# Matrix-memory layer of a three-part decoder: gates as rows, convolution beside the gate branch, heads normalised from PSUM; attention transposes through four banks

## Reference

```python
def mlstm_mixer(u, w_in, conv_w, conv_b, wq, wk, wv, w_gates, b_gates, norm_w, skip, w_out):
    xm, z = jnp.split(u @ w_in, 2, axis=-1)                 # 2048 wide each
    xc = jax.nn.silu(causal_depthwise_conv(xm, conv_w, conv_b))   # 4 taps
    q, k, v = block_diag_proj(xc, wq), block_diag_proj(xc, wk), block_diag_proj(xm, wv)
    gates = q @ wg_q + k @ wg_k + v @ wg_v + b_gates        # 6144 -> 8: 4 heads, i and f
    i_pre, f_pre = jnp.split(gates, 2, axis=-1)
    log_f = jax.nn.log_sigmoid(f_pre)
    h = mlstm_chunkwise(...)       # running sum and running maximum of the gates over the tokens,
                                   # decay matrix from them, scores q k^T times decay, times v,
                                   # divided by max(|row sum|, exp(-m))
    # each head of 512: (h - mean) * rsqrt(var + eps), per token
    h = (h * norm_w + skip * xc) * jax.nn.silu(z)
    return h @ w_out
```

## Time and profile before

| | |
|---|---|
| median of 3 runs | 3438.85 us (3420.95 to 3454.4) |
| the profiled execution | 3429.66 us, of which the span of instructions 3427.9 us |
| PE busy | 3193.9 us, 93% of the span |
| DVE, ACT busy | 1022.8 us (30%), 473.2 us (14%) |
| DMA | 732.26 MB, mean 214 GB/s |
| mean granted clock of TensorE | 0.959 of full speed |

### The profile page before, as it was taken

The page is one execution under the profiler, slowest core; times in us unless marked ns, Lnnn a source line. Parts: engine busy times, 40 slices in busy tenths (PEclk is TensorE's granted clock), DMA queues, the critical chain, the costliest instruction groups (busy, mean ns, idle before and its releaser), DMA issues.

```text
span 3427.9 us, 56270 instructions
## 1 busy us (share of the span) xinstructions
PE 3193.9 (93%) x24082; PEld 2691.2 (79%) x24083; DVE 1022.8 (30%) x2204; ACT 473.2 (14%) x1077; POOL 15.1 (0%) x26
## 2 busy tenths in 40 slices
PE   5999999999999999999998768997679999999998
PEld 4888888888888888888887757886666887668875
DVE  5213222320221322242035253368431111111113
ACT  1001112100100111210001200005320111101110
POOL 0000000000000000000000000000000000000000
PEclk8999999999999999999999669999889999999999
DMA  8646534364464563436446205760329788898884
GB/s 331 245 160 250 197 130 178 123 246 184 156 260 162 212 230 136 178 123 245 184 160 258 101 0 188 300 262 1 125 95 353 298 325 318 314 352 326 329 320 189
DMA packets 55190, 732.26 MB, mean 214 GB/s; under 512 B 6576, under 2 KB 6760, under 8 KB 10516
## 3 DMA queue, kind: packets, MB, share of 16 engines
q1 hardware_dynamic: 51092, 716.69, 54.7%
q0 software_dynamic: 3968, 13.74, 1.2%
HBM read 729.32 MB, written 4.23 MB: 214 GB/s over the span
## 4 chain that ended last, share of the span: by engine, by line
PE 81%; DMA 8%; DVE 7%; issue 2%; ACT 1%; SPq 0%; DVEq 0%; POOL 0%; ACTq 0%; POOLq 0%
PE psum L639 48%; PE psum L1041 11%; PE psum L1084 9%; PE psum L626 2%; PE psum L696 2%; DMA ring<-in_up_dram 2%; DMA ring<-in_up_e_dram 2%; DVE ring L1424 2%; PE psum L817 1%; PE psum L1065 1%; PE psum L1100 1%; DMA ring<-in_down_e_dram 1%; DMA ring<-in_w_qk_dram 1%; DVE work L1943 1%; DMA ring<-in_ada_dram 1%
## 5 line engine op out<-in xcount | busy, mean ns | idle before, releaser
L639 PE MATMUL psum<-h_t,ring 128*128 128x256 f32 x5888 | 1291.6, 382 | 31.2 <-DVE h_t L1570 8.8
L639 PEld LDWEIGHTS psum<-h_t,ring 128*128 128x128 f32 x5888 | 1124.3, 191 | 197.6 <-issue 29.0
L639 PE MATMUL psum<-work,ring 128*128 128x256 f32 x2752 | 603.4, 382 | 21.8 <-ACT work L1255 10.2
L639 PEld LDWEIGHTS psum<-work,ring 128*128 128x128 f32 x2752 | 526.7, 192 | 96.8 <-ACT work L1255 10.6
L1041 PE MATMUL psum<-h_t,ring 128*64 128x96 f32 x11264 | 471.7, 247 | 5.9 <-DMA ring<-in_up_e_dram 5.6
L1041 PEld LDWEIGHTS psum<-h_t,ring 128*64 128x64 f32 x11264 | 467.8, 137 | 9.1 <-issue 7.8
L1084 PE MATMUL psum<-ring,work 128*96 128x512 f32 x704 | 304.1, 593 | 0.6 <-DMA ring<-in_down_e_dram 0.5
L1424 DVE SCALAR_TENSOR_TENSOR ring<-ring,cond 128x1024 f32<-128x1024 f32 x240 | 279.2, 1220 | 36.5 <-DMA ring<-in_ada_dram 35.4
L1084 PEld LDWEIGHTS psum<-ring,work 128*96 128x96 f32 x704 | 114.1, 163 | 184.9 <-issue 183.1
L1487 DVE TENSOR_TENSOR work<-work,psum 128x256 f32<-128x256 f32 (+1 forms) x118 | 49.7, 421 | 624.2 <-PE psum L639 609.3
L2235 DVE TENSOR_TENSOR work<-work,psum 128x256 f32 x176 | 74.2, 421 | 403.8 <-PE psum L1041 403.8
(11 more groups left out here) (326 smaller groups left out, 1652.2 us busy)
## 6 DMA issues: line engine op xcount, KB each, us to landing
ring<-in_up_e_dram SPq DMA_DIRECT2D x64, 2048.0 KB, 7.7
ring<-in_ada_dram SPq DMA_DIRECT2D x60, 2048.0 KB, 7.8
ring<-in_up_dram SPq DMA_DIRECT2D x55, 2048.0 KB, 7.9
ring<-in_down_e_dram SPq DMA_DIRECT2D x32, 1792.0 KB, 8.5
ring<-in_down_dram SPq DMA_DIRECT2D x20, 2816.0 KB, 9.6
ring<-in_up_e_dram SPq DMA_DIRECT2D x32, 1536.0 KB, 8.4
ring<-in_down_e_dram SPq DMA_DIRECT2D x16, 2048.0 KB, 8.9
ring<-in_w_qk_dram SPq DMA_DIRECT2D x12, 2048.0 KB, 8.6
```

Of the source, the lines that this page charges most:

```text
L639: mm = pe.matmul(half(b), w, moving(k, j * lin.groups + m), start=(k == 0), stop=(k == depth - 1))
```

## The change

Matrix-memory mixer: z has no ada chunks; `m_out` has four instead (with one chunk of its own ahead). DVE makes the convolution in four parts of four tiles during z, and ACT puts silu of part j-1 behind z's chunk j, of the last two parts behind chunk 3. The gate products come before `vtok`: the gate weights (128x4, input or forget gates) are stationary and the 128x256 activation tiles move; four results, for two tiles and two gates, go to partitions 0, 32, 64, 96 of bank 4. Weights and `tri` are fetched at the start of z, into `rms` and `skip`; the rows lie in `h`. ACT copies three of the four partial rows, DVE adds them. The skip scaling of `xc` stands ahead of the gates on DVE. PE's order is then `vtok`, scores of heads 0 and 1, `rows_t`, scores of heads 2 and 3. In the numerator PE goes head by head; DVE takes statistics straight from PSUM, and ACT writes (h - mean) * scale from PSUM (`Identity` with bias and scale). Head transposes go to banks 4 to 7, the product with silu(z) is made tile by tile, and `m_out` waits for one tile at a time. Attention: the transposes rotate through banks 4 to 7, and each v product waits for its own head.

```diff
-    mix = uses(b4=4, b5=4, b6=1, b7=1)
+    mix = uses(b4=2, b5=2, b6=3, b7=3)
...
-        "xm": Linear(4, 4, 32 * P, "m_xm", 4, 1, biased=4), "z": Linear(4, 4, 32 * P, "m_z", 4),
+        "xm": Linear(4, 4, 32 * P, "m_xm", 4, 1, biased=4), "z": Linear(4, 4, 32 * P, "m_z"),
...
-        "m_out": Linear(4, 2, 32 * P, "m_out"), "ln0": ln_after,
+        "m_out": Linear(4, 2, 32 * P, "m_out", 4, 1), "ln0": ln_after,
...
                 for n in range(HG):
-                    b = 4 + n % 2
+                    b = LIN + n % LIN
                     pe.wait_ge(signal["probs"], lp.of("probs", n + 1))
-                    pe.wait_ge(bank_free[b], reads(p, b, n // 2))
+                    pe.wait_ge(bank_free[b], reads(p, b, n // LIN))
...
-                pe.wait_ge(bank_free[4], reads(p, 4, 4))
-                pe.wait_ge(bank_free[5], reads(p, 5, 4))
-                pe.wait_ge(bank_free[6], reads(p, 6))
-                pe.wait_ge(bank_free[7], reads(p, 7))
+                pe.wait_ge(bank_free[6], reads(p, 6, 2))
                 for n in range(HG):
                     e = (g * HG + n) * HD
+                    pe.wait_ge(bank_free[LIN + n % LIN], reads(p, LIN + n % LIN, n // LIN) + 1)
...
+            p = place("gates")
+            pe.wait_ge(mgate_in, 48)
...
+            for pair in range(3 * MT // 2):
...
+                for part in range(2):
+                    k = 2 * pair + part
+                    src = (mq, mk, mvt)[k // MT][:, k % MT, :]
+                    w = w_gate_m[k // 32][:, k % 32, :]
+                    for n in range(2):
+                        lo = 32 * (2 * part + n)
+                        mm = pe.matmul(psum[lo:lo + MH, 4 * 512:4 * 512 + S], w[:, n * MH:(n + 1) * MH], src,
+                                       start=(pair == 0), stop=(pair == 3 * MT // 2 - 1))
+            mm.then_inc(signal["full4"], 1)
...
+            scores((0, 1))
+            rows_out_t()
+            scores((2, 3))
...
+            numerator(0)
+            denominators()
+            numerator(1)
+            numerator(2)
+            heads_out(0)
+            numerator(3)
+            for n in range(1, MH):
+                heads_out(n)
+            linear(place("m_out"), lambda k, n: mh[:, k, :], reads_k=lambda k: (signal["mh"], place("h_t").of("mh", k + 1)))
...
+            for j in range(4):
+                for m in range(4):
...
+                    act.activation(zs[:, 4 * j + m, :], half(b), ACT.Silu).then_inc(bank_free[b], 1)
+                if j:
+                    conv_out_act(j - 1)
+            conv_out_act(3)
...
+            for n in range(MH):
+                act.wait_ge(signal["mvar"], p.of("mvar", n + 1))
+                act.activation(by_head(var_m)[:, :, n], by_head(var_m)[:, :, n], ACT.Sqrt).then_inc(signal["mroot"], 1)
+                if n:
+                    normalised(n - 1)
+            normalised(MH - 1)
...
             for n in range(MH):
+                variance(n)
+                if n:
+                    scale_of(n - 1)
+            scale_of(MH - 1)
...
+            def gate_heads(f):
+
+                dve.wait_ge(dve_done, steps.count(but=0 if f == MT - 1 else 1))
+                dve.tensor_tensor(mh[:, f, :], mh[:, f, :], zs[:, f, :], ALU.mult).then_inc(signal["mh"], 1)
...
-            take_second(place("m_out"), 2 * DT, 6 * DT)
-            scale_x()
-            add_to_x(place("m_out"), mod1[:, 2 * DT:3 * DT], place("ln0"))
+            p = place("m_out")
+            walk(p, loop(p), add_chunk(p, mod1[:, 2 * DT:3 * DT], place("ln0")), ada_sums(p))
+            ada_next(p, (mod_next[:, 4 * DT:6 * DT], vec[:, rest + 2 * DT:rest + 4 * DT], 2 * DT))
+            take_second(place("ln0"), 4 * DT, 6 * DT)
...
-                pool.wait_ge(bank_free[b], reads(place("gates"), b))
-            pool.dma_start(w_gate_m, dram["m_gates"]).then_inc(mgate_in, 16)
+                pool.wait_ge(bank_free[b], reads(place("z"), b))
+            pool.dma_start(w_gate_m[0], dram["m_gates"][:, 0:32, :]).then_inc(mgate_in, 16)
+            pool.dma_start(w_gate_m[1], dram["m_gates"][:, 32:48, :]).then_inc(mgate_in, 16)
```

More of the change, by code:

```diff
@@ L819, in _ @@
[L819 to L835, removed]
-            mm.then_inc(signal["full4"], 1)
-            for b in (5, 6):
-                pe.wait_ge(bank_free[b], reads(p, b))
-                for n in range(2):
-                    hd = (b - 5) * 2 + n
-                    mm = pe.matmul(half(b, n), ident[0:MH, hd:hd + 1].to_broadcast([MH, P]), row(4), start=True, stop=True)
-                mm.then_inc(signal[f"full{b}"], 1)
@@ L862, in _, with scores @@
-            mm.then_inc(signal["full7"], 1)
-            for n in range(MH):
+            def scores(heads):
+                p = place("scores")
+                for n in heads:
+                    pe.wait_ge(bank_free[n], reads(p, n))
+                    for c, (a, z, lo) in enumerate(((0, P, 0), (P, S, P))):
+                        for k in range(4):
+                            mm = pe.matmul(bank(n)[:, c * S:c * S + S - lo], mk[:, 4 * n + k, a:z],
+                                           mq[:, 4 * n + k, lo:S], start=(k == 0), stop=(k == 3))
+                    mm.then_inc(signal[f"full{n}"], 1)
@@ new lines, in rows_out_t @@
+            def rows_out_t():
+                pe.wait_ge(signal["rows"], place("gates").of("rows", 1))
+                p = place("rows_t")
+                pe.wait_ge(bank_free[4], reads(p, 4))
+                for n in range(2):
+                    for t in range(TT):
+                        c = 4 * 512 + n * 8 + t * MH
+                        mm = pe.transpose(psum[:, c:c + MH], row(5 + n)[:, t * P:(t + 1) * P],
+                                          ident[0:MH, 0:MH])
+                mm.then_inc(signal["full4"], 1)
+                for b in (5, 6):
+                    pe.wait_ge(bank_free[b], reads(p, b))
+                    for n in range(2):
+                        hd = (b - 5) * 2 + n
+                        mm = pe.matmul(half(b, n), ident[0:MH, hd:hd + 1].to_broadcast([MH, P]), row(4), start=True, stop=True)
+                    mm.then_inc(signal[f"full{b}"], 1)
@@ L1260, in _ @@
                          act.activation(dst[:, m, :], ps, ACT.Copy))
+            p = place("gates")
+            act.wait_ge(bank_full[4], products(p, 4))
+            for k, lo in ((4, 64), (5, 96), (6, 32)):
+                e = act.activation(row(k), psum[lo:lo + MH, 4 * 512:4 * 512 + S], ACT.Copy)
+            e.then_inc(signal["gate_rows"], 1)
+            act.wait_ge(signal["gate_size"], p.of("gate_size", 1))
+            act.activation(row(2), row(2), ACT.Exp, scale=-1.0).then_inc(act_done, steps.one())
+            act.wait_ge(act_done, steps.count())
+            act.activation(row(2), row(2), ACT.Ln, bias=1.0).then_inc(signal["gate_logs"], 1)
             p = place("vtok")
@@ L1265, in _ @@
                     act.activation(mv[:, t, b * 512:(b + 1) * 512], bank(b), ACT.Copy).then_inc(bank_free[b], 1)
-            p = place("gates")
-            act.wait_ge(bank_free[5], reads(p, 5, 0) + 1)
-            act.activation(row(2), row(1), ACT.Abs).then_inc(act_done, steps.one())
-            act.wait_ge(act_done, steps.count())
-            act.activation(row(2), row(2), ACT.Exp, scale=-1.0).then_inc(act_done, steps.one())
-            act.wait_ge(act_done, steps.count())
-            act.activation(row(2), row(2), ACT.Ln, bias=1.0).then_inc(signal["gate_logs"], 1)
             p = place("rows_t")
@@ L1510, in add_to_x, with add_chunk, chunk @@
             def add_to_x(p, scale, after):
+                for j in range(p.what.chunks):
+                    add_chunk(p, scale, after)(j, 0, p.slot(j))
+            def add_chunk(p, scale, after):
                 lin = p.what
-                for j in range(lin.chunks):
+                def chunk(j, i, where):
                     for m in range(lin.groups):
@@ L1816, in _ @@
             for name, dst in (("q", mq), ("k", mk), ("vT", mvt)):
                 evacuate(place(name), range(1, 16, 2), lambda j, m, i, ps: dve.tensor_copy(dst[:, m, :], ps))
-            p = place("vtok")
-            for t in range(TT):
+            for f in range(MT):
+                dve.tensor_scalar(xc[:, f, :], xc[:, f, :], vcol("mlstm_skip_2", f), None, ALU.mult).then_inc(dve_done, steps.one())
+            p = place("gates")
+            dve.wait_ge(bank_full[4], products(p, 4))
+            dve.wait_ge(signal["gate_rows"], p.of("gate_rows", 1))
```

295 lines of the change are left out of this document (152 added, 143 removed).

## The result

The changed kernel took 3335.27 us (median of 4 runs, 3329.69 to 3339.85) against 3433.39 us (4 runs, 3420.95 to 3454.4): ratio 0.9713, 95% interval 0.9681 to 0.9744, 98 us less. In a later batch it gave 3332.73 us and 0.9719 (0.969 to 0.9749). Its profiled execution took 3336.4 us, with a span of 3334.6; the one before had 3427.9, so the traces differ by 93.3 us.

The account below looks back on a forecast made before the run. PE, busy 93% of the span, was taken as the bound. Mixer terms sum to 223.9 against 297.7 us (−73.8), attention −10: 3429.66 − 83.8 = 3345.9, plus half of a 9.2 us profile-to-median gap, 3350 us (3322 to 3386).

Parts of the forecast that it names:

- z: Product z without ada chunks: PE's wait before it 7.8 to 0.2 us, the product 57.4 to 55.8 us.
- q, k, vT: Products after z: 23.2 to 21.7 us, allowing half of the slow start after a 3.8 us pause.
- Gates: Gate products: four strips overlap at full clock, 41.2 to 11 us, and the 8.5 us idle before them goes.
- In order: Rival for the gates: records start only in program order, so 20.9 us, +10 to 3360; chance 0.12.
- half clock: Rival for the gates: four stationary columns bring half clock, gates 21 us and slow vtok, +14 to 3364; chance 0.10.
- vtok over the gate chain: After the gates: vtok and scores cover the 8.8 us of small steps; vtok 9.1 us, scores with `rows_t` 12.8.
- Numerator to `m_out`: From the end of the scores to `m_out`, head by head: 40.7 to 32.2 us, bounds 28 to 38.
- Layer norm: After `m_out`: DVE's fourth ada chunk adds 4.4 us of PE waiting, 15.3 to 19.7 us (18 to 21).
- Attention: Six attention mixes with four transpose banks: 1.7 us less each, 10 us in all (5 to 15).
- Short covers: Rival for the head loop: four handover waits of 1.5 us and a decay 3 us late, +9 to 3359; chance 0.12.
- Attention gives nothing: Rival for the attention: DVE and ACT copies set the pace, no gain, +10 to 3360; chance 0.04.
- Draining strips: Rival for the gates: strips don't overlap and each change drains, gates 124 us, +113 to 3463; chance 0.03.

Follow-up runs that it names:

- experiment 5: The changed kernel with the four ada chunks back in z and none in `m_out`: 3339.43 us, ratio 0.9723.
- run 11: The changed kernel again, unaltered, in a later batch: 3332.73 us, ratio 0.9719 to the kernel before.
- experiment 7: The changed kernel with ACT's silus of the last two convolution parts put between the evacuations of z's last chunk: 3327.75 us, ratio 0.9704.
- experiments 2 to 4: The changed kernel with the gate products reordered: two strips by turns, eight records in a row per strip, strip after strip; 3342.78, 3350.72 and 3366.01 us.
- experiment 3: The changed kernel with eight gate records in a row on one strip, then the next strip: 3350.72 us.
- experiment 6: The changed kernel with each ada chunk in `m_out` read one chunk earlier, none left for the end: 3331.75 us, ratio 0.9709.
- experiments 1 and 9: The changed kernel with the attention's transposes back on two banks, 3356.46 us (0.9784); the kernel before with the four banks alone, 3409.2 us (0.9919).
- experiment 4: The changed kernel with all gate products of one strip before those of the next: 3366.01 us.
- experiments 8 and 12: The changed kernel with ada chunks and silus early and vtok's first two banks emptied between the exp and ln steps: 3318.18 us, then again 3320.55 us.

## Why the prediction was right, step by step

Predicted 3350, measured 3335. The sum for the mixer was 223.9 us, the trace has 223.7. The mechanisms were right, but that the sums agree to 0.2 us is luck: the layer norm is 2.6 us over its term and q, k, vT 0.9, against 1.8 under in the numerator, 0.8 in `m_out`, 0.6 in the gates and 0.5 in z. Of the 15 us of the total, 6.3 come from the attention, 3.0 from behind `up3`, and 5 from what was added for the median. In order:

- **z.** Wait 0.2 → 0, z 55.8 → 55.3. Right, and for the named reason: z's chunks stand in SP's queue ahead of the time they are needed; with ada back the wait is 8.5 again (experiment 5). In run 11 a wait of 0.93 us for z's first chunk was left, inside the 0 to 1.5 allowed.
- **Convolution beside z.** Pause 3.8 → 3.7: eight silus and one evacuation (3.58 us of ACT in the third row of the table). Right, and avoidable (experiment 7).
- **q, k, vT.** 21.7 → 22.6. I allowed half of the slow start, 0.8 us. A pause of 3.7 us costs 1.8 to 2.7 (20.9 without any pause, 22.7 or 23.6 with it), against 2.3 after the 10.2 us of before.
- **Gates.** 11 → 10.4, clock 1.00. Four at a time was right in size, and experiments 2 to 4 show it by its own scale (39.0, 20.0, 10.4). The fetch of weights and `tri` costs PE nothing: the gates begin as vT ends. That, and vtok over the steps behind the gates, is read from the trace; no experiment takes either back alone. "In order" would have given 20.9 and is refuted, and so is half clock. What I leaned on was weaker than I took it: I read the earlier trace rows as a look-ahead that doesn't care for runs of eight, and experiment 3 gives 21.9 for such runs. The number stood because this order changes the strip after every second record. By the Trainium skill ("TensorE: Matmul & The Clock Gate", Part 3) matmuls start in program order, and its factor for four row strips is 3.07. The first does not hold in these runs (21.9 us in experiment 3 where such an order needs 36, and 10.4 instead of some 21 in the changed kernel); the factor, here for strips of columns, is 3.7 to 4.0.
- **vtok over the gate chain.** 9.1 → 9.2 with a wait of 1.61 us on ACT (L1317), and scores with `rows_t` 12.8 → 13.0. Right; the decay was never waited for.
- **Numerator to `m_out`.** 32.2 → 30.4. The pauses of the heads are 2.8, 2.0 and 2.6 us; I said 2.7 and 1.5 and then folded the last transposes into DVE's tail (29 and 3 are 32.0, not the 32.2 of the sum). DVE's sixteen pairs took 13.6 us, 0.85 each as summed.
- **m_out with ada.** 57.6 → 56.8; no chunk landed late.
- **Layer norm.** 19.7 → 22.3. The wait grew by 4.4, as worked out. The weak step is "15.3 → 19.7", which added the wait to an otherwise unchanged stretch: after 6.0 us without work PE resumes at a granted clock of 0.57, and the sums of squares take 2.7 us longer (experiment 6 takes both away, run 11 has both again).
- **Attention.** −10 → −16.3 in the profiled execution, beyond the far end of its range (15). Other executions have more: with four banks xm ends between 1794.0 and 1802.8 us in twelve, against 1818.7 before. Two terms were mis-sized. A mix gives 2.3 us, not 1.7 (13.8 for six): I had bank 6 hold up the v products until DVE's copy of head 6 ends "near 3.9", and the first v product starts at 3.28 with a wait of 0.32. The other part is the clock of the first mix, which the prediction had only as the far end of its range: it was full in twelve of twelve profiled executions with four banks, and in one of two with two banks.
- **From `up3` on.** 0 → −3.0. No edit of these kernels lies there, and the stretch took 1305.7 to 1317.3 us in the fourteen profiled executions (1308.5 and 1310.8 for the changed kernel), so this is spread.
- **Profiled run against median.** I put 4 us on top of the sum; the after run was 1 us above its median.
- **The other rivals.** Short covers: the decay isn't late and the pauses of the heads are near those counted. Attention gives nothing: experiments 1 and 9 have 2.3 us in each mix. Draining strips: the gates would have taken 124 us. All are out.
- **A slip without effect.** "Half of it is the gates": by the prediction's own terms it is 46.5 of 73.8 us, nearly two thirds.

## What to carry to other kernels

Thin results that don't fill the array belong in strips of partitions of one PSUM bank, with the large operand moving, and with the strip changing from product to product: the order alone was worth a factor of two (10.4 against 21.9 us). When a stream of work is moved away from one stage, follow it to the end of its new stage: there the ada passes cost 7.0 of the 11.5 us that their move had saved, until they were started one chunk earlier. And price a pause of PE of several microseconds twice, once as time and once as the clock of the thin work behind it.

## What the runs showed of the hardware

- Records of 4 stationary and 256 moving columns on different strips of one bank: 216 ns each one after the other on one strip, 104 ns with two strips by turns, 54 with four, 114 with four strips in runs of eight.
- At a change from a busy strip to another, four records of the next strip start beside the last four of the one before, whether the run before it was 8 records long (experiment 3) or 48 (experiment 4).
- The granted clock stayed at 1.00 through 39 us of products that use 4 of 128 stationary columns, where 41 us of products with 8 moving columns, behind a pause of 8.5 us, sat at 0.50 throughout.
- After about 6 us without work PE's next 16 records took 5.1 to 6.6 us instead of 3.7, in eight executions of eight. After 3.7 us of pause 96 records took 1.8 us longer in five executions and 2.7 in four.
- Where the clock drops isn't fixed by the kernel alone: mixes with two banks had it at 0.50 in part of one execution and at 1.00 in another, and 16 records behind a wait of 1.6 us took 3.69 us in experiment 6 and 5.38 in experiments 8 and 12.
